# A two-layer trunk with expert retrieval: the prompt's first choice cut by heads, its state stored through SyncE's queue, and early weights dealt anew

## What is computed

```python
q = (xb @ w_q).reshape(128, 8, 2, 128)                  # 8 heads, 2 half queries
s = einsum('tphd,phnd->tphn', q, subkeys)               # 128 keys for each half
s1, i1 = top_k(s[:, :, 0], 16); s2, i2 = top_k(s[:, :, 1], 16)
cand = s1[..., :, None] + s2[..., None, :]              # 256 pairs
top, pos = top_k(cand, 16)                              # 16 experts a head
eidx = take_along_axis(i1 * 128 + i2, pos)              # of 16384 experts
act = gelu(einsum('tped,td->tpe', u[eidx], xb))
out = einsum('tpe,tped->td', softmax(top) * act, v[eidx])
```

## Time and profile before

| | |
|---|---|
| median of 3 runs | 2360.69 us (2354.72 to 2361.48) |
| the profiled execution | 2356.56 us, span of the core 2354.7 us, granted clock 0.82 |
| busy in the span | PE 67%, DVE 67%, ACT 36%, POOL 37% |
| moved by DMA | 956.47 MB, mean 406 GB/s; 805.36 MB of them gathers |
| DMA, 20 us stretches of 400 to 540 us | 419 to 422 GB/s |

### The profile page before, as it was taken

One profiled execution on the slowest core, in us unless ns is written; L12 is line 12 of the kernel. 1 busy time (PEld: TensorE's weight loads), 2 busy tenths in 40 slices (PEclk: granted clock), 3 DMA queues, 4 the chain that ended last, 5 costly groups with the idle time before them and its releaser, 6 DMA issues. The chain is left out here.

```text
span 2354.7 us, 28968 instructions
## 1 busy us (share of the span) xinstructions
PE 1570.0 (67%) x9366; PEld 838.0 (36%) x9366; DVE 1567.8 (67%) x4321; ACT 840.2 (36%) x2750; POOL 859.9 (37%) x772
## 2 busy tenths in 40 slices
PE   8887977786865445656646677788767545555554
PEld 6775733664521112324512344455433102101010
DVE  2357988556777876565697567765875897665654
ACT  2324445523323223343233435543432334222232
POOL 0013344323334243333335333343544444444341
PEclk9998988898877678778878798898877777776777
DMA  9979999999999999999999999999999999999996
GB/s 387 408 267 399 368 394 412 421 421 402 420 421 421 421 421 421 421 420 401 420 421 392 418 421 420 374 421 421 415 420 422 421 421 421 421 422 421 422 422 269
DMA packets 144858, 956.47 MB, mean 406 GB/s; under 512 B 17732, under 2 KB 20420, under 8 KB 35652
## 3 DMA queue, kind: packets, MB, share of 16 engines
q0 software_dynamic: 110592, 805.36, 82.6%
q1 hardware_dynamic: 28784, 144.94, 15.2%
q10 hardware_dynamic: 5332, 4.33, 0.8%
HBM read 951.67 MB, written 2.89 MB: 405 GB/s over the span
## 5 line engine op out<-in xcount | busy, mean ns | idle before, releaser
L821 POOL DMA_INDIRECT rows<-in_uv,eidx x768 | 859.6, 1119 | 1454.8 <-PE acc L909 1083.2
L1471 DVE CUSTOM_DVE_ANT_0 rows<-rows,xrep 128x1024 f32<-128x1024 f32 x768 | 913.9, 1224 | 410.4 <-DMA rows<-in_uv,eidx 407.6
L909 PE MATMUL acc<-rows,diag 128*32 128x512 f32 x3072 | 763.6, 745 | 529.4 <-ACT diag L1161 513.6
L909 PEld LDWEIGHTS acc<-rows,diag 128*32 128x32 f32 x3072 | 154.0, 126 | 1029.6 <-ACT diag L1161 674.9
L1161 ACT ACTIVATE act_out<-act_in 128x2 f32<-128x2 f32 x384 | 77.8, 203 | 983.9 <-DVE act_in L1471 983.4
L839 PE MATMUL bank<-wt,hT 128*128 128x256 f32 x888 | 209.3, 397 | 24.7 <-DMA wt<-in_attn_w_qkv 8.1
L1161 ACT ACT_TABLE_LOAD x120 | 154.0, 1283 | 171.3 <-DVE act_in L1471 86.0
L1161 ACT ACTIVATE diag<-small,wv 128x32 f32<-128x32 f32 x768 | 204.8, 314 | 12.5
L839 PEld LDWEIGHTS bank<-wt,hT 128*128 128x128 f32 x888 | 175.8, 200 | 66.6 <-issue 19.9
L839 PE MATMUL bank<-hT,wt 128*128 128x256 f32 (+1 forms) x896 | 179.8, 363 | 14.9 <-DMA wt<-in_peer_w_q 8.2
L1161 ACT ACTIVATE wv<-act_out,gate 128x1 f32<-128x1 f32 x768 | 184.2, 287 | 12.6
(11 more groups left out here) (177 smaller groups left out, 1365.8 us busy)
## 6 DMA issues: line engine op xcount, KB each, us to landing
wt<-in_ada_w SPq DMA_DIRECT2D x24, 1024.0 KB, 9.6
wt<-in_peer_w_q SPq DMA_DIRECT2D x24, 1024.0 KB, 9.5
rows<-in_ada_w SPq DMA_DIRECT2D x36, 512.0 KB, 15.1
wt<-in_mlstm_w_in SPq DMA_DIRECT2D x12, 1024.0 KB, 9.0
rows<-in_uv,eidx POOLq DMA_INDIRECT x768, 22.6
wt<-in_attn_w_qkv SPq DMA_DIRECT2D x12, 1024.0 KB, 9.4
rows<-in_mlstm_w_in SPq DMA_DIRECT2D x21, 512.0 KB, 16.1
rows<-in_peer_w_q SPq DMA_DIRECT2D x16, 512.0 KB, 13.7
```

Source lines behind the costliest of these rows:

```text
L821: nc.gpsimd.indirect_dma_start(out=rows[:, r, :], out_offset=None, in_=A["uv"], in_offset=bass.IndirectOffsetOnAxis(ap=eidx[:, b, slot:slo ...
L909: last = nc.tensor.matmul(acc[c:c + QUAD, h * 512:(h + 1) * 512], diag[:, r, :], rows[:, r, D + h * 512:D + (h + 1) * 512], start=first, s ...
L1471: last = V.tensor_tensor_reduce(out=rows[:, r, 0:D], in0=rows[:, r, 0:D], in1=xrep[:, GS * odd + j, :], scale=1.0, scalar=0.0, op0=ALU.mul ...
```

## The change

1. The first quarter is chosen by heads instead of by token halves. `PQ` of it is cut into two steps of one weight tile (one head each), `PS` into two of one head with all 128 tokens on the partitions. Expert numbers of a head are moved between quadrants by 16 operations instead of 8, and POOL is told after the eighth (group 0) and after the sixteenth. `PW` weighs both heads at once, also by 16. Scores and pairs of this choice lie in spare parts of `eidx` and `gate`, so it no longer waits for the stores.
2. `MLU` comes behind the queries and the first head's choice. The six stores of the state are issued by SP behind the 99 early loads (after waiting for DVE's copies of MLU) instead of by ACT. DVE waits for them ahead of PS of the third quarter.
3. The adaLN tiles `mod(1, 0)` and PS of the second quarter run ahead of XR and of the first group. PQ of the third and fourth quarter stay behind it.
4. The early loads fill `rows` first and `wt` last (`LAP`), and the last early load is PQ of the fourth quarter; the last five places, those in `wt`, are then held by PS of the third quarter and PQ of the fourth.
5. The statistics of the sample's first norm are a step of their own (`STAT`) behind the prompt's MLN; its two NORM steps write into `hm` and stand ahead of the second quarter's choice, its NT steps inside it.
6. `DEALS` and `PATIENCE` of the first 64 groups are new.

```diff
-    yield from (("NT", 0, 1, 0), *cell(["MLU"], 0), *cell(["MLU"], 1), ("STATE",))
-    yield from (("PQ", 0, "P", 0), ("PS", 0, "P", 0, 0), ("PQ", 0, "P", 1), ("XR", 0, 0, 0), ("XR", 0, 0, 1))
-    yield from ((k, 0, "P", 0, 0, half) for half in range(2) for k in ("PT", "PC", "PG"))
-    yield from (("PW", 0, "P", 0, 0, half) for half in range(2))
-    rest = [("PS", 0, "P", 0, 1), ("PQ", 0, "P", 2), ("PS", 0, "P", 0, 2), ("PQ", 0, "P", 3), *mod(1, 0)]
+    yield ("NT", 0, 1, 0)
+    for head in range(2):
+        yield from (("PQ", 0, "P", 0, head), ("PS", 0, "P", 0, 0, head))
+    yield from (("PQ", 0, "P", 1), ("PT", 0, "P", 0, 0, 0), ("PC", 0, "P", 0, 0, 0), ("PG", 0, "P", 0, 0, 0))
+    yield from (*cell(["MLU"], 0), *cell(["MLU"], 1), *mod(1, 0))
+    yield from (("PT", 0, "P", 0, 0, 1), ("PC", 0, "P", 0, 0, 1), ("PG", 0, "P", 0, 0, 1), ("PS", 0, "P", 0, 1))
+    yield from (("XR", 0, 0, 0), ("XR", 0, 0, 1), ("PW", 0, "P", 0, 0))
+    norms, turned = ([(k, 0, 0, b) for b in BLOCKS["S"]] for k in ("NORM", "NT"))
...
-    start = [*quarter[1], ("PS", 0, "P", 0, 3), *later[0:6], *quarter[2], *later[6:9], *quarter[3]]
+    start = [*norms, ("PQ", 0, "P", 2), quarter[1][0], ("PS", 0, "P", 0, 2), ("PQ", 0, "P", 3), quarter[1][1], *turned, quarter[1][2],
+             ("PS", 0, "P", 0, 3), *later[4:6], *quarter[2], *later[6:9], *quarter[3]]
...
+LAP = [*range(WRING, EARLY), *range(WRING)]
-    last_early = PLAN.index(("MR", 1, 0, 3))
+    last_early = PLAN.index(("PQ", 0, "P", 3))
-                    load(src[:, c:min(c + HALF * WC, n)], len(loads) % EARLY, last)
+                    load(src[:, c:min(c + HALF * WC, n)], LAP[len(loads) % EARLY], last)
...
+                if n == EARLY_LOADS:
+                    for d in range(2):
+                        last = of(("MLU", "P", d, 0)) + MH - 1
+                        sp.wait_ge(by(last), emptied(last))
+                        sp.dma_start(O["new_C"][0, 0, d].rearrange("h p v -> p h v"), cell("P", d)[2][:, :, 0:DV]).then_inc(state_out, 16)
+                        sp.dma_start(O["new_n"][0, 0, d].rearrange("h p -> p h"), cell("P", d)[2][:, :, DV], allow_slow_non_contiguous=True).then_inc(state_out, 16)
+                        sp.dma_start(O["new_m"][0, 0, d:d + 1, :], mst[0:1, d, :]).then_inc(state_out, 16)
...
-                    if g % QG == 0 or g == QG // 2:
-                        pool.wait_ge(experts_chosen, g // QG + 1 + (g > 0))
+                    if g % QG == 0 or g in (1, QG // 2):
+                        pool.wait_ge(experts_chosen, g // QG + 1 + (g > 0) + (g > 1))
...
+                elif k == "STAT":
+                    act.wait_ge(sample_in, 16)
+                    rsqrt_parts([x[:, b, :] for b in BLOCKS["S"]], Nflat[:, 0:D], KEPT)
...
+                    if s == ("PS", 0, "P", 0, 2):
+
+                        dve.wait_ge(state_out, 96)
...
+                    if half:
+                        chosen = [e12[:, a, n].rearrange("p (j k) -> p k j", k=QUADS) for a in range(2)]
+                        experts = eidx[:, blk, n].rearrange("p (j q) -> p q j", q=QUADS)
+                        for q in range(QUADS):
+                            for kk in range(QUADS):
+                                last = V.scalar_tensor_tensor(experts[quadrant(kk), q], chosen[0][quadrant(q), kk], 1.0 / PACK,
+                                                              chosen[1][quadrant(q), kk], ALU.mult, ALU.add)
+                            if q == QUADS - 1 or (q == 1 and half == [0]):
+                                last.then_inc(experts_chosen, 1)
+                        continue
```

More of the change, by code:

```diff
@@ L227, in plan @@
     quarter = {q: [(k, 0, "P", 0, q) for k in ("PT", "PC", "PG")] for q in others}
-    start = [*quarter[1], ("PS", 0, "P", 0, 3), *later[0:6], *quarter[2], *later[6:9], *quarter[3]]
+    start = [*norms, ("PQ", 0, "P", 2), quarter[1][0], ("PS", 0, "P", 0, 2), ("PQ", 0, "P", 3), quarter[1][1], *turned, quarter[1][2],
+             ("PS", 0, "P", 0, 3), *later[4:6], *quarter[2], *later[6:9], *quarter[3]]
     later = [s for s in later if s not in start]
-    yield from spread(0, 0, [*rest, *start, *later[:-3], *among([*later[-3:], *norm(0, 1, "S"), *choice(0, "S", 0, first, True)], mod(0, 5))])
+    yield from spread(0, 0, [*start, *later[:-3], *among([*later[-3:], *norm(0, 1, "S"), *choice(0, "S", 0, first, True)], mod(0, 5))])
     yield from spread(0, 1, among([*choice(0, "S", 0, others, True), *choice(0, "S", 1, every, False)],
@@ L242 @@
 PLAN = list(plan())
-FIRST_SCORES = ("PS", 0, "P", 0, 0)
+FIRST_SCORES = [("PS", 0, "P", 0, 0, head) for head in range(2)]
 ROOT_FIRST = [("MLN", "P", 0), ("NORM", 0, 1, 0), ("YOUT", 2)]
@@ L638, in trunk @@
         loads, last_use = weight_loads(A)
+        EARLY_LOADS = sum(place < EARLY for _, place, _, _ in loads)
         rows_in = [sem(f"rows_in{i}") for i in range(RING * GS)]
@@ L878, in by_token, with by_feature @@
                         product(t[:, 0:WC], lambda k: hT[:, k, tok(b)], lambda k: w(k)).then_inc(tile_full, 1)
-            def by_feature(n_tokens):
-                for j in range(2):
+            def by_feature(n_tokens, tiles=2):
+                for j in range(tiles):
                     if j:
@@ L1091, in _ @@
                 elif k == "PQ":
-                    by_feature(P * len(BLOCKS[s[2]]))
+                    by_feature(P * len(BLOCKS[s[2]]), 1 if len(s) > 4 else 2)
+                elif s in FIRST_SCORES:
+                    if s == FIRST_SCORES[0]:
+                        _, place, turn, _ = loads[used[0]]
+                        used[0] += 1
+                        first_keys = weight_place(place)
+                        pe.wait_ge(w_in[place], 16 * turn)
+                    t = open_tile(0)
+                    for a in range(2):
+                        e = 2 * s[5] + a
+                        last = mm(t[:, a * NKEYS:(a + 1) * NKEYS], qTp[:, e, 0:P], first_keys[:, e * NKEYS:(e + 1) * NKEYS], True, True)
+                    last.then_inc(tile_full, 1)
                 elif k == "PS":
@@ L1174, in rsqrt_parts @@
                         act.wait_ge(act_chain, noted())
-                    last = f(out, src, ACT.Square, accum_out=ssq[:, b:b + 1])
+                    last = f(out, src, ACT.Square, accum_out=ssq[:, at + b:at + b + 1])
                     if b < n - 1:
@@ L1355, in _ @@
                 elif k == "PQ":
-                    _, l, g, q = s
+                    _, l, g, q, *head = s
                     n = P * len(BLOCKS[g])
-                    for i in range(4):
-                        copy_tile(i, qTp[:, 4 * q + i, 0:n], n)
+                    first = 4 * q + 2 * sum(head)
+                    for i in range(2 if head else 4):
+                        copy_tile(i, qTp[:, first + i, 0:n], n)
                 elif k == "XR":
@@ L1825, in _ @@
                     last.then_inc(experts_chosen, 1)
-                    if not half:
-                        weigh(s)
+                    weigh(s)
                 elif k == "AN":
```

129 lines of the change are left out of this document (74 added, 55 removed), and 2 rows, old and new, of the table DEALS.

## The result

The changed kernel takes 2366.09 us (median of 22 runs, 2356.96 to 2379.62), the kernel before 2359.66 us beside it (22 runs, 2353.75 to 2365.33). The ratio is 1.003, interval 1.0019 to 1.0041: slower by 6.4 us, where I had forecast 10.6 us faster. The profiled execution took 2369.93 us, with a span of 2368.1.

The account below looks back on a forecast made before the run. DMA was taken as the bound, time won only where it runs dry: -1.9 + 3.1 + 7.5 + 1.9 = 10.6 us off 2356.56 gives 2346.0 profiled, 2350 for the median; range 2341 to 2363.

Parts of the forecast that it names:

- the price of the stores: State stores sharing DMA engines with gathers cost 5 us, between 2.5 (bytes alone) and 9.1 (all their queue's busy time).
- the stores hold DVE: Rival, chance 0.08: DVE waits for the stores ahead of PS 2's scores, if they land after about 205; 2370 us.
- one-in-between: One gather packet between any two store packets: 36.6 us, stores done near 197, a 9 us wait that slack swallows.
- The first gap: Between early reads and first gathers: 22.4 us shrinks to 19.3, less 5 for stores, net -1.9 (bounds +0.6, -6.0).
- First gather near 153: POOL's first gather goes at 153.0 instead of 161.16 us, with no wait of DVE for a store ahead.
- Reads end near 135: The early loads end near 135.5 us instead of 141.1, as 2.25 MB (5.6 us) come later.
- Stores issued by SP near 157: SP issues the state stores near 157 us, after DVE's copies of MLU, instead of from 137.75.
- STAT: The sample's statistics on ACT, ahead of the output gates, delay the chain 0.5 us, bounds 0 and 2.5.
- XR to 171.5, PQ 2 ends 179 to 181.5: PE behind the first scores: XR (7.2 us) ends about 171.5, PQ 2 at 179 to 181.5, the first sum then too.
- The later holes: DMA dips behind 220 us: the 7.5 us of 220 to 260 go, and 1.9 of 300 to 320 come back.
- POOL's longest wait: Sign in the changed profile: under 15 us, where it was 23.23 us for a sum by PE.
- The half of 300 to 320: Half of the 3.7 us DMA loses at 300 to 320 us is won, 1.9, as DVE is busy.

Follow-up runs that it names:

- a_again: The changed kernel unaltered, measured again for a second profile; 2363.47 us, 1.0019 to the kernel before.
- a_xr: The changed kernel with XR ahead of the adaLN tiles (C and n stored are other numbers); 2380.11 us, 1.0102 to the kernel before.
- a_third: The changed kernel unaltered, on another chip; 2379.1 us, 1.0089 to the kernel before.
- a_fourth: The changed kernel unaltered, in the last series, on another chip; 2375.57 us, 1.0072 to the kernel before.
- a_mlu_first: The changed kernel with MLU back ahead of the first queries, so the stores go into the dry stretch; 2348.56 us, 0.9955 to the kernel before.
- a_row_fourth: The changed kernel with n stored as two runs of 2 KB behind m, in the last series; 2352.01 us, 0.9972 to the kernel before.
- a_row_stat: The changed kernel with n stored as two runs of 2 KB and STAT moved ahead of the output product; 2353.37 us, 0.9983 to the kernel before.
- a_mlu_fourth: The changed kernel with MLU back ahead of the first queries, in the last series; 2348.45 us, 0.996 to the kernel before.
- a_mlu_xr: The changed kernel with MLU ahead of the first queries and XR ahead of the adaLN tiles; 2354.13 us, 0.9986 to the kernel before.
- a_n_row: The changed kernel with n made a row by PE and stored as two runs of 2 KB behind m; 2354.44 us, 0.9994 to the kernel before.
- a_no_n: The changed kernel without the two stores of n, that output not written; 2356.49 us, 0.9999 to the kernel before.
- a_mlu_third: The changed kernel with MLU back ahead of the first queries, a third time; 2349.61 us, 0.9968 to the kernel before.
- a_no_state: The changed kernel without the four stores of C and n, only m stored; 2357.02 us, 0.9998 to the kernel before.
- a_mlu_again: The changed kernel with MLU back ahead of the first queries, repeated on another chip; 2359.25 us, 1.0004 to the kernel before.
- a_first_row: The changed kernel with MLU ahead of the first queries and n stored as two runs of 2 KB; 2361.77 us, 1.0011 to the kernel before.
- the third series: Runs measured together on one chip: `a_no_state`, `a_mlu_again` and `a_first_row`; ratios to the kernel before 0.9998, 1.0004 and 1.0011.
- a_no_c: The changed kernel without the two stores of C, that output not written; 2359.37 us, 1.0006 to the kernel before.

## Why the prediction was wrong

**The step that failed first is the price of the stores.** I took 5 us with bounds of 2.5 (their bytes) and 9.1 (all that their queue had been busy). In 180 to 220 us the loss was 10 to 13 in the five profiled executions of such kernels, above the upper bound, and the 2.5 us of their bytes come on top. The error is in the method: I priced the stores by their own packets' time, and packets of 4 bytes among gathers lengthen the gathers' packets, from 281 to 411 ns over 40 us and to 517 ns where they stand alone beside them. n's 1024 packets are 64 turns of an engine; at 517 instead of 272 ns a turn that is 16 us by this estimate. The row was also taken from a stretch where only reads stood beside them, whose share of 1.18 at 201 GB/s already hinted at occupied engines that move little.

**The second is the rival to which I gave 0.08: the stores hold DVE.** I had its place (PS 2), its point (landing after about 205) and nearly its price (2370), and let one-in-between, "done near 197", decide. One-in-between is what the traces show, 254 packets to 253 and 151 to 151; the length of a turn was wrong. I counted 132 turns of 0.277 us, 36.6 us; by the turns measured, 68 of 0.272 and 64 of 0.517, they are 51.6, and from the first store's issue to VectorE's copy it took 46 to 58. So it is the same mis-sized term once more. In the five profiled executions of kernels with C, n in elements and m all among the gathers the wait behind them was:

| kernel | first issue | copy at PS 2 | between | wait for the store | ScalarE stood | profiled execution | ratio of medians |
|---|---|---|---|---|---|---|---|
| `a_again` | 156.67 | 202.59 | 45.9 us | 2.35 us | 7.67 us | 2358.33 us | 1.0019 |
| first result | 164.90 | 212.50 | 47.6 us | 4.41 us | 7.73 us | 2369.93 us | 1.003 |
| `a_xr` | 164.99 | 221.54 | 56.6 us | 22.80 us | no | 2379.36 us | 1.0102 |
| `a_third` | 166.39 | 224.11 | 57.7 us | 24.15 us | no | 2379.60 us | 1.0089 |
| `a_fourth` | 160.81 | 218.64 | 57.8 us | 24.29 us | no | 2376.09 us | 1.0072 |

The last landing thus lay between 202 and 224, on both sides of the point I had named. Small holds go with ratios near 1.002, large ones with 1.007 to 1.010. The small holds are just those of the two executions in which ScalarE stood. There POOL ran out of places for 17 to 18 us (its wait ends at 192.60 in `a_again`, at 199.57 in the first result), and in the 5 us from 190 and from 200 DMA moved 446 and 553 packets under 512 bytes, against 253 at most in such a stretch of `a_third`: the stores got through where few gathers were left, and the late chain brought VectorE to PS 2 later. That this makes the hold small is argued from two executions against three, and why ScalarE stands in some series and not in others was not found. That such a difference also makes the 23 us of spread in the first result, whose 22 runs reach from the one case to the other, is argued, not shown: only one of them was profiled.

**The first gap.** "First gather near 153" held in six profiled executions (152.77 to 153.29 us, `a_again` and `a_mlu_first` among them); in seven it was 154.67 to 158.49, in five 160.19 to 162.71, and in none did a store hold VectorE ahead of it. In the first result it was 161.20: the clock was 0.50 from 135 to 145, and the first head's queries took 6.59 us instead of 3.74; `a_third` (162.71) and `a_row_fourth` (161.23) show the same. That is not all of the 8.2 us by which the first gather is behind `a_again`'s: PE's order of time is 3.4 us behind at 39 us, 4.5 at 88, and 3.7 come between 129 and 149. The windows of the earlier trace rows show 1.00 there, and the forecast put the term at nothing. Reads end near 135 in `a_again`, as forecast; in the first result SP's last early issue begins at 129.50, and 138 GB/s still move in 135 to 140. "Stores issued by SP near 157" came at 156.7 in `a_again` and at 164.90 in the first result, by the same delay.

**STAT** costs 0.3 us (PE's order of time in the first result is 3.2 us behind the kernel before's ahead of it and 3.5 behind it; it was 3.5 behind at 39 us already), my 0.5. Moving it, `a_row_stat`, changed nothing that can be told.

**The chain behind the scores.** "XR to 171.5, PQ 2 ends 179 to 181.5" holds in `a_mlu_first` (180.30) and `a_mlu_fourth` (172.46 + 7.41 = 179.87), where the first dot product is at 172.76. In the first result PQ 2 ends at 202.87: 8 us from the first gather, 7.7 of ScalarE's standing, and XR over 14.1 us instead of 7.2. I costed XR from a row in which DMA was dry, but full DMA alone does not slow it: in `a_fourth`, among gathers, it takes 7.4 us of products with a wait for VectorE of 1.7 between them. That its place mattered was refuted by `a_xr` and `a_mlu_xr`.

**The later holes.** 220 to 260 closed as forecast in the first result (420 and 419 GB/s), though the total got worse; in the three executions with a long hold 2.0 to 9.8 us were lost there. In `a_mlu_first` and `a_mlu_fourth` the sample's first MLQK begins at 206.25 and 207.21 and POOL goes on at 224.53 and 223.80, where the forecast had 206 to 208 and 225: that part of the mechanism stands. POOL's longest wait was 19.33 us, not under 15, and fell to 15.04 in `a_mlu_fourth`. The half of 300 to 320 did not come: 326 GB/s, and in the repaired kernels a larger hole stands at 280 to 300 (279 to 285 GB/s in `a_n_row`, `a_no_n` and `a_row_fourth`). It lies over the last of the sample's four long products (275.68 to 290.51 in `a_n_row`), and the deal tried against it gained nothing. In `a_mlu_fourth` it is 367 GB/s.

**The sum, by what was measured.** By 220 us the forecast had 29.9 us lost (31.1 before, less 3.1, plus 1.9). It was 50.0 in the first result, 41.5 in `a_again`, 31.1 without n and 30.3 with n in runs. With the stores moved into the dry stretch the kernel comes near the forecast: `a_mlu_first`, `a_mlu_third` and `a_mlu_fourth` are 8.1, 7.8 and 9.5 us under the kernel before of their series, beside the forecast's 10.6, and `a_row_fourth`, in the forecast's own order, 6.0. Where ScalarE stood there was no gain: `a_no_n`, `a_n_row`, `a_no_state`, `a_mlu_again` and `a_first_row`, which all avoid n's elements among gathers, are between 0.9994 and 1.0011. The changed kernel itself puts 10 to 13 us of slowed transfers and a hold of 2 to 24 us on top.

**What stays open.** What makes ScalarE stand for 7.6 us: the kernels of the third series, all with it, are at 0.9998 to 1.0011, and `a_mlu_again`'s loss at 640 us is 49.7 us against 33.9 in `a_mlu_first`. Of these 15.8 us 8.1 lie ahead of 180 us, with the late first gather, so the wait and what follows it are worth 8 us at most in this pair; no run here takes it away. No version that beats these was found: the best is MLU ahead of the queries, faster than the kernel before in three series of four (in the third 1.0004), and than the changed kernel beside it in the two that had both.

## What to carry to other kernels

Price a transfer of tiny elements by what it does to the transfers beside it, not by its own busy time or its bytes; if it cannot be written as rows, send it where DMA is dry anyway. Freeing an engine of a wait by moving the stores later made them last three times as long, and the wait came back at the next reader of the buffer. When a rival's deciding point lies inside the uncertainty of the number that decides it, its chance is not 0.08. And run one kernel in several series, on more than one chip, before trusting a difference of ten microseconds.

## What the runs showed of the hardware that I had not expected

- Beside packets of 4 bytes the gathers' packets of 8 KB took 517 ns, beside packets of 1 KB 272 ns, with one packet of the one queue to one of the other both times (`a_fourth`).
- The second issue of 512 elements of 4 bytes on SyncE's queue took 10.8 to 12.1 us among gathers, and that of m behind it, 16 bytes, another 8 to 12; with the stores in the dry stretch (`a_mlu_fourth`) 0.51 and 1.01. It takes C's stores too: in `a_no_c` both issues of n among gathers took 0.40 us. In the kernel before, on ScalarE's queue, the issues of n and m took 0.52 to 1.15 us.
- The C stores (1 MB) lay between 168.5 and 204.9 us in the first result and between 137.6 and 150.9 in `a_mlu_first`.
- One program on one core took 2363, 2366, 2376 and 2379 us in four comparisons, and `a_mlu_first`'s program 2348, 2349, 2350 and 2359, while the kernel before stayed within 2356.7 and 2359.7.
- TensorE's granted clock differs between executions of one kernel at the same place. It was 0.50, 0.50, 0.65 in the three windows of 15 to 30 us in the first result and 0.57, 0.50, 0.90 in `a_again`; at 39 us PE was 3.4 us behind in the first. From 129 to 149 us, at 0.50 up to 145 against 0.66 in 135 to 140 and 1.00 else, it fell behind by 3.7 more.
